# A22 copies in two PSUM banks by turns, block sums joined in SBUF ahead of the weight sums, later row sums, and regrouped last rows

## The chip, the core and the metric

The kernel runs on one core of one Trainium2 chip. The metric is the device time of one execution in microseconds; the kernel before takes 2215.24 us, the median of three runs. TensorE is called PE, VectorE DVE, ScalarE ACT, GpSimd POOL and SyncE SP. Every matmul operand is float32, cut into a rounded high part and a low part (the rest), and each product is three matmuls: high by high, low weight by high, high weight by low.

## The reference, cut to what matters

Two layers over 512 tokens of width 1024. Each layer has two gated feed-forward blocks (FFN) around a mixing stage; the FFNs are what the change touches.

```python
def swiglu(x, w_in, w_out):
    a, b = jnp.split(x @ w_in, 2, axis=-1)
    return (jax.nn.silu(a) * b) @ w_out

for l in range(DEPTH):                      # DEPTH = 2
    h = h + 0.5 * swiglu(rmsnorm(h, ffn1_norm[l]), ffn1_w_in[l], ffn1_w_out[l])   # D_FF = 2816
    u = rmsnorm(h, mix_norm[l])
    ...                                     # three branches, one of them attention into mem
    y_c = mem_attention(q_c, rmsnorm(mem, mem_norm[l]), w_mem_kv[l])
    ...
    h = h + 0.5 * swiglu(rmsnorm(h, ffn2_norm[l]), ffn2_w_in[l], ffn2_w_out[l])
return rmsnorm(h, final_norm)
```

## The kernel before, in words

**Pairs.** An FFN computes its 22 hidden tiles of 128 (both halves, so 44 units of weights) and its output as a list of 30 pairs, FLOW. A pair of kind "S" (four, at the front) is computed the standard way: two units of 24 matmuls over 512 tokens. The other 26 are computed by a fast product of 2 x 2 blocks: seven block products of 12 matmuls over 256 tokens each, 84 matmuls in all, in the order of PRODUCTS: A11, A12, S2, S1, S3, A22, S4. The A's are quarters of the weights and the S's are sums of quarters. Kind "K" is a hidden tile, kind "O" two output tiles whose result is added to h. The order is 4 S, 4 K of group A, 1 K of group C, 4 O, 8 K of group B, 1 K of C, 4 O, 4 K of C. The hidden tiles of groups A and B go in couples (tile t and tile t + 4, which I call near and far): their sums, sumS, are what the O pairs multiply. The last six hidden tiles (group C) are multiplied in the standard way by outs(), eight units of 18 matmuls over 512 tokens, into bank[k % 4].

**Windows.** PE runs pair after pair. On ACT and DVE, window(last, now, then) holds what belongs beside pair now: the end of pair last, the middle of now, and the weights of then. What stands in a window is in program order; all waits are on semaphores. In DVE's window: finish_blocks(last) (block sums from bank[1..3] into obank and bank[3], and the scaling by rms), then gate(last) or add_rows(last), then low_late A22 (the low part of now's A22 weights), low(last), low_late S4, sum_two and sum_four (weight sums of then), mix_first(now) (the first block sums of now, in obank and ta), low_s2, add_mem (only in the first FFN of a layer, after an O pair: squares of mem are added up), mix_two(now), couple_sums(last).

**Banks and who waits for them.** PE may begin the next pair's A11 and A12 when mix_first has read bank[0] and bank[1] (semaphore mixed), S1 when finish_blocks has read bank[2] (crossed), A22 when low(last) or add_rows is done (pair_done). The quarter A22 of the coming pair is copied by ACT into the PSUM bank tbank (copy_a22, line 1491), where sum_two and the rounding and low part of A22 read it; the copy waits for late_low, that is for both low_late steps of the pair before, since they read the bank.

**POOL and SP.** For every fast pair POOL makes two weight sums and four low parts (lines 842, 836, 848, 836), and after each second tile of a couple two low parts of the couple's sums (line 859). SP loads the quarters in the order A11, A12, A21, A22; A12 waits for sum_four.

**Last rows.** After outs() unit k, DVE's last_row(k) adds the result to h, makes the low part for the next stage, copies the row back to h and adds its square, which ACT makes, to ssq. norm_mem and low_mem (mem for the memory attention) stand after row 0 and row 1. PE's units k + 4 and, after them, the memory units wait for the bank of row k.

## Time and profile before

| | before |
|---|---|
| median of 3 runs | 2215.24 us (2213.0 to 2216.5) |
| profiled execution | 2214.67 us |
| span in the profile | 2212.9 us |
| granted clock of TensorE, mean | 0.992 |
| PE busy | 2141.6 us, 97% of the span |
| PE weight loads busy | 1928.8 us, 87% |
| DVE busy | 1678.9 us, 76% |
| POOL busy | 1490.8 us, 67% |
| ACT busy | 1068.6 us, 48% |
| DMA | 213.18 MB, mean 96 GB/s |

The table says how full each engine is over the whole program. The profile's waits say on whom PE waited, and the rows in order of time say how long one window of DVE is compared with one pair of PE. The stage from 56 to 341 us is the first FFN of layer 0 with its fast pairs, 802 to 1072 us its second FFN; the last rows of the first FFN lie from 341 to 394 us, and layer 1 repeats all of it some 1093 us later.

### The profile page before, as it was taken

The numbers are of one execution on the slowest core, as the hardware profiler recorded it, in microseconds if no ns is written. First come the engines' busy times: TensorE is split into PE (matmuls) and PEld (weight loads), VectorE is DVE, ScalarE is ACT, GpSimd is POOL, SyncE is SP. The second block draws the span as 40 slices with busy tenths as digits, with TensorE's granted clock in tenths as the row PEclk, the third lists the DMA queues.
The fourth block names the chain that finished last, engine by engine and source line by source line (L and its number), as shares of the span: only waits on it lengthen the run. The fifth ranks groups of instructions, "written<-read, shape, count | busy, mean of one in ns | idle before, by whom it ended". The sixth has DMA issues, their size and how long they took to land. (4 is left out here: it accounts for less than half of the span.)

```text
span 2212.9 us, 39425 instructions
## 1 busy us (share of the span) xinstructions
PE 2141.6 (97%) x13990; PEld 1928.8 (87%) x13990; DVE 1678.9 (76%) x3116; ACT 1068.6 (48%) x2067; POOL 1490.8 (67%) x1094
## 2 busy tenths in 40 slices
PE   9999998999999999999999999989999999999997
PEld 6999997788888889999879999968788888999996
DVE  6888887568765588888778888865787555888884
ACT  5545542444554255564345455434445533555552
POOL 6877866544445678788768788765444466788874
PEclk9999999999999999999999999999999999999999
DMA  5332333322222323333323233332222133232232
GB/s 167 108 109 92 115 106 110 116 70 67 72 63 77 106 85 101 107 99 101 109 82 117 96 101 114 109 121 93 69 63 72 54 108 96 81 111 97 98 104 85
DMA packets 95235, 213.18 MB, mean 96 GB/s; under 512 B 10400, under 2 KB 13640, under 8 KB 94792
## 3 DMA queue, kind: packets, MB, share of 16 engines
q1 hardware_dynamic: 90864, 205.42, 28.7%
q10 hardware_dynamic: 4184, 5.31, 0.7%
q8 instruction: 112, 1.84, 0.3%
q14 instruction: 75, 0.61, 0.1%
HBM read 208.58 MB, written 3.68 MB: 96 GB/s over the span
## 5 line engine op out<-in xcount | busy, mean ns | idle before, releaser
L791 POOL TENSOR_SCALAR wH<-raw 128x1024 fp32r<-128x1024 f32 (+2 forms) x184 | 173.4, 942 | 422.3 <-PE bank L921 352.3
L794 POOL TENSOR_TENSOR wL<-raw,wH 128x1024 fp32r<-128x1024 f32 (+2 forms) x184 | 389.1, 2115 | 15.3
L1051 PE MATMUL bank<-u1H,wH 128*128 128x256 f32 x1152 | 330.8, 287 | 10.3 <-DVE far4L L2031 6.3
L1052 PE MATMUL bank<-u1H,wL 128*128 128x256 f32 x1152 | 327.1, 284 | 0.0
L1053 PE MATMUL bank<-u1L,wH 128*128 128x256 f32 x1152 | 327.0, 284 | 0.0
L836 POOL TENSOR_TENSOR wL<-wS,wH 128x512 fp32r<-128x512 f32 x208 | 273.1, 1319 | 74.3 <-ACT wH L1497 39.3
L836 POOL TENSOR_TENSOR wL<-raw,wH 128x512 fp32r<-128x512 f32 x208 | 280.5, 1369 | 2.2 <-ACT wH L1503 2.1
L919 PE MATMUL bank<-u1H,wH 128*128 128x512 f32 x704 | 281.6, 400 | 0.0
L920 PE MATMUL bank<-u1H,wL 128*128 128x512 f32 x704 | 275.0, 391 | 0.0
L921 PE MATMUL bank<-u1L,wH 128*128 128x512 f32 x704 | 274.8, 390 | 0.0
L1051 PE MATMUL bank<-u0H,wH 128*128 128x256 f32 x864 | 248.3, 287 | 9.4 <-DVE ta L1959 9.1
L1052 PE MATMUL bank<-u0H,wL 128*128 128x256 f32 x864 | 244.4, 283 | 0.0
L1053 PE MATMUL bank<-u0L,wH 128*128 128x256 f32 x864 | 244.3, 283 | 0.0
L1051 PEld LDWEIGHTS bank<-u1H,wH 128*128 128x128 f32 x1152 | 222.1, 193 | 16.0 <-DVE far4L L2031 7.1
L1052 PEld LDWEIGHTS bank<-u1H,wL 128*128 128x128 f32 x1152 | 222.3, 193 | 0.0
L1053 PEld LDWEIGHTS bank<-u1L,wH 128*128 128x128 f32 x1152 | 222.1, 193 | 0.0
L842 POOL TENSOR_TENSOR wS<-raw 128x512 f32<-128x512 f32 x104 | 134.9, 1297 | 107.9 <-issue 89.5
L1051 PEld LDWEIGHTS bank<-u0H,wH 128*128 128x128 f32 x864 | 165.4, 191 | 16.8 <-DVE ta L1959 16.0
L1503 ACT ACTIVATE wH<-raw 128x512 fp32r<-128x512 f32 x208 | 130.3, 629 | 84.8 <-PE bank L1053 84.8
L1052 PEld LDWEIGHTS bank<-u0H,wL 128*128 128x128 f32 x864 | 165.6, 192 | 0.1
L1053 PEld LDWEIGHTS bank<-u0L,wH 128*128 128x128 f32 x864 | 165.5, 192 | 0.0
L919 PEld LDWEIGHTS bank<-u1H,wH 128*128 128x128 f32 x704 | 132.4, 188 | 33.4 <-issue 7.4
(332 smaller groups left out, 6113.4 us busy)
## 6 DMA issues: line engine op xcount, KB each, us to landing
raw<-in_wA SPq DMA_DIRECT2D x296, 256.0 KB, 2.9
raw<-in_wM SPq DMA_DIRECT2D x96, 512.0 KB, 3.5
raw<-in_wO SPq DMA_DIRECT2D x128, 256.0 KB, 2.9
raw<-in_wA SPq DMA_DIRECT2D x28, 512.0 KB, 3.6
raw<-in_wC SPq DMA_DIRECT2D x32, 384.0 KB, 3.0
raw<-in_wR SPq DMA_DIRECT2D x32, 256.0 KB, 2.6
keep<-in_memT SPq DMA_DIRECT2D x4, 512.0 KB, 3.3
mem<-in_memT SPq DMA_DIRECT2D x2, 1024.0 KB, 7.5
```

The lines of the kernel that those rows point to most:

```text
L791: pool.tensor_scalar(wH[:, w, 0:cols], raw[:, slot, 0:cols], 1.0, 0.0, ALU.mult, ALU.add).then_inc(rounded, 1)
L794: pool.tensor_tensor(wL[:, w, 0:cols], raw[:, slot, 0:cols], wH[:, w, 0:cols].bitcast(F32), ALU.subtract).then_inc(split_done, 1)
L836: pool.tensor_tensor(half_slot(wL_flat, n), full, half_slot(wH_flat, n).bitcast(F32), ALU.subtract).then_inc(pool_low, 1)
L842: pool.tensor_tensor(half_slot(wS, weights_at("S3", g)), quarter("A11"), quarter("A21"), ALU.subtract).then_inc(pool_sum, 1)
L919: pe.matmul(dst, a, hi[:, k, :], start=first and i == 0, stop=False)
L920: pe.matmul(dst, b, hi[:, k, :], start=False, stop=False)
L921: mm = pe.matmul(dst, a, lo[:, k, :], start=False, stop=last and i == len(tiles) - 1)
L1051: pe.matmul(dst, a, hi, start=begin and k == 0, stop=False)
L1052: pe.matmul(dst, b, hi, start=False, stop=False)
L1053: mm = pe.matmul(dst, a, lo, start=False, stop=end and k == 3)
L1503: act.activation(half_slot(wH_flat, weights_at(name, g)), quarter(name), ACT.Copy).then_inc(k_rounded, 1)
```

## The change

It does five things.

1. copy_a22 copies into tbank for even pairs and into obank for odd ones (a22_bank). The copy waits only for the A22 low part of the pair two before, and stands earlier in ACT's window, ahead of high(last) and copy_first(now).
2. Block sums are joined in SBUF. copy_first writes to sg instead of ta; mix_first is one operation over 512 columns into ta instead of two over 256 into obank and ta; finish_blocks sums one half into ta (SBUF), multiplies ta by rms there, and makes both crossed halves with one operation over two banks (banks_two). bank[2] and bank[3] change places: S1 and S3 go to bank[3], A22 and S4 to bank[2].
3. mix_first comes ahead of sum_two and sum_four in DVE's window.
4. A near tile stays in sumS itself, and the couple's sums are three operations instead of four. They stand ahead of low_s2. Those of the four standard pairs come in the windows at positions 3 and 4, and their high and low parts at 4 and 5.
5. In last_row the square of row k - 1 is added after the first operation of row k (add_square); norm_mem comes after row 1 instead of 0, low_mem after row 3 instead of 1, and ACT's parts of them after rows 1 and 2. A wait of PE on k_scaled is dropped.

```diff
+def couples_due(now, last):
+    if now is not None and now.pos in (4, 5):
+        return [FLOW[2 * (now.pos - 4) + 1]]
+    return [last] if last is not None and last.kind == "K" and last.group in "AB" and last.at >= 4 else []
...
         def kept(p):
-            return keep[:, p.at // 4, :]
+            return keep[:, p.at % 2, :] if p.at >= 4 else sumS[:, 2 * p.at, :]
+
+        def a22_bank(g):
+            return (tbank, obank)[g % 2]
...
-        bank = [ctx.enter_context(nc.psum_tensor(f"bank{i}", [P, 512], F32)) for i in range(BANKS)]
+        bank = [ctx.enter_context(nc.psum_tensor(f"bank{i}", [P, 512], F32)) for i in range(BANKS - 2)]
+        banks_two = ctx.enter_context(nc.psum_tensor("banks_two", [P, 2, 512], F32))
+        bank += [banks_two[:, i, :] for i in range(2)]
...
                         act.wait_ge(quarter_landed["A22"], 16 * (g + 1))
-                        act.wait_ge(late_low, 2 * g)
-                        act.activation(tbank[:, :], quarter("A22"), ACT.Copy).then_inc(a22_copied, 1)
+                        if g >= 2:
+                            act.wait_ge(late_low, 2 * (g - 2) + 1)
+                        act.activation(a22_bank(g)[:, :], quarter("A22"), ACT.Copy).then_inc(a22_copied, 1)
...
-                        act.activation(ta[:, 0:TH], bank[0][:, 0:TH], ACT.Copy).then_inc(first_copied, 1)
+                        act.activation(sg[:, 0, 0:TH], bank[0][:, 0:TH], ACT.Copy).then_inc(first_copied, 1)
...
                         if seven_then:
                             round_quarter(then, "A12")
+                            copy_a22(then)
                         if last is not None and last.kind != "O":
                             high(last)
                         if seven_now:
                             copy_first(now)
                         if seven_then:
-                            copy_a22(then)
                             round_sum(then, "S3")
...
-                        own.done(dve.tensor_tensor(obank[:, 0:TH], bank[1][:, 0:TH], ta[:, 0:TH], ALU.add))
-                        dve.tensor_tensor(ta[:, TH:T], bank[1][:, TH:T], ta[:, 0:TH], ALU.add).then_inc(mixed, 1)
+                        dve.tensor_tensor(halves(ta[:, :]), halves(bank[1][:, :]), twice(sg[:, 0, 0:TH]), ALU.add
+                                          ).then_inc(mixed, 1)
...
-                        own.done(dve.tensor_tensor(obank[:, TH:T], bank[3][:, TH:T], sg[:, 1, 0:TH], ALU.add))
-                        own.done(dve.tensor_tensor(bank[3][:, 0:TH], bank[3][:, 0:TH], sg[:, 1, TH:T], ALU.add))
+                        own.done(dve.tensor_tensor(ta[:, TH:T], bank[2][:, TH:T], sg[:, 1, 0:TH], ALU.add))
                         own.wait()
+                        scaled_rows = dve.tensor_tensor(ta[:, :], ta[:, :], rms[:, :], ALU.mult)
...
-                        dve.tensor_tensor(bank[3][:, TH:T], bank[2][:, 0:TH], sg[:, 1, TH:T], ALU.add
+                        dve.tensor_tensor(halves(bank[2][:, :]), banks_two[:, :, 0:TH], twice(sg[:, 1, TH:T]), ALU.add
                                           ).then_inc(crossed, 1)
...
-                        for i, made in ((0, obank), (1, bank[3])):
+                        for i, made in ((0, ta), (1, bank[2])):
...
+                        near, cross, own_two = sumS[:, 2 * j, :], sumS[:, 2 * j + 1, :], kept(p)
                         if p.at < 4:
-                            dve.tensor_tensor(sumS[:, 2 * j, left], keep[:, 0, right], keep[:, 0, left], ALU.subtract
+                            dve.tensor_tensor(near[:, left], near[:, right], near[:, left], ALU.subtract
                                               ).then_inc(couple_sum, 1)
                             return
-                        dve.tensor_tensor(sumS[:, 2 * j + 1, right], keep[:, 1, right], keep[:, 0, right], ALU.subtract
+                        dve.wait_ge(couple_sum, n + 1)
+                        dve.tensor_tensor(halves(cross), twice(own_two[:, right]), halves(near), ALU.subtract
                                           ).then_inc(couple_sum, 1)
-                        dve.tensor_tensor(sumS[:, 2 * j + 1, left], keep[:, 1, right], sumS[:, 2 * j, left], ALU.subtract
-                                          ).then_inc(couple_sum, 1)
...
+                        if seven_now:
+                            mix_first(now)
                         if seven_then:
                             sum_two(then)
                             sum_four(then)
-                        if seven_now:
-                            mix_first(now)
+                        if now is not None and now.pos in (3, 4):
+                            for p in FLOW[2 * (now.pos - 3):2 * (now.pos - 3) + 2]:
+                                couple_sums(p)
+                        if last is not None and last.kind == "K" and in_couple(last):
+                            couple_sums(last)
                         if seven_then:
                             low_s2(then)
...
-                        if last is not None and in_couple(last):
-                            couple_sums(last)
...
-                    finish_h(k, bank[k % BANKS][:, :], sbank[k % 2][:, :], 0.5, l * 24 + k + (n_from + 1), g, hi, lo)
+                    dve.scalar_tensor_tensor(ps, ps, 0.5, h[:, k, :], ALU.mult, ALU.add).then_inc(h_added, 1)
+                    if k:
+                        add_square(k - 1, n - 1)
```

The order on DVE in one window after an O pair, in the first FFN of layer 0, before (bank3, bank2: the PSUM banks; sbank0 and sbank1 hold weight sums):

```order
L1975 TENSOR_TENSOR obank<-bank3,sg 128x256
L1976 TENSOR_TENSOR bank3<-bank3,sg 128x256
L1981 TENSOR_TENSOR obank<-obank,rms 128x512
L1982 TENSOR_TENSOR bank3<-bank2,sg 128x256
L1989 TENSOR_TENSOR bank3<-bank3,rms 128x512
L1993 SCALAR_TENSOR_TENSOR h<-obank,h 128x512
L1993 SCALAR_TENSOR_TENSOR h<-bank3,h 128x512
L1938 TENSOR_TENSOR wL<-tbank,wH 128x512
L1938 TENSOR_TENSOR wL<-sbank1,wH 128x512
L1916 TENSOR_TENSOR sbank0<-tbank,wS 128x512
L1924 TENSOR_TENSOR sbank1<-raw,sbank0 128x512
L1958 TENSOR_TENSOR obank<-bank1,ta 128x256
```

And the same window in the changed kernel:

```order
L1989 TENSOR_TENSOR ta<-banks_two,sg 128x256
L1991 TENSOR_TENSOR ta<-ta,rms 128x512
L1996 TENSOR_TENSOR banks_two<-banks_two,sg 128x512
L2003 TENSOR_TENSOR banks_two<-banks_two,rms 128x512
L2007 SCALAR_TENSOR_TENSOR h<-ta,h 128x512
L2007 SCALAR_TENSOR_TENSOR h<-banks_two,h 128x512
L1952 TENSOR_TENSOR wL<-obank,wH 128x512
L1952 TENSOR_TENSOR wL<-sbank1,wH 128x512
L1972 TENSOR_TENSOR ta<-bank1,sg 128x512
L1930 TENSOR_TENSOR sbank0<-tbank,wS 128x512
L1938 TENSOR_TENSOR sbank1<-raw,sbank0 128x512
L1945 TENSOR_TENSOR wL<-sbank0,wH 128x512
```

The block sum of the current pair (L1958, now L1972) has moved ahead of the two weight sums, the operations of a window are two fewer, and two of them (L1991 and the first L2007) now have both inputs in SBUF.

The order on ACT from the first rounding of a window to the copy of the first block, after a far tile (raw: the quarters as loaded; wH: rounded weights), before:

```order
L1517 ACTIVATE wH<-tbank 128x512
L1503 ACTIVATE wH<-raw 128x512
L1523 ACTIVATE sg<-ta 128x512
L1517 ACTIVATE wH<-sbank1 128x512
L1503 ACTIVATE wH<-raw 128x512
L1537 ACTIVATE far4H<-keep 128x512
L1530 ACTIVATE ta<-bank0 128x256
L1491 ACTIVATE tbank<-raw 128x512
```

And in the changed kernel:

```order
L1530 ACTIVATE wH<-tbank 128x512
L1516 ACTIVATE wH<-raw 128x512
L1537 ACTIVATE sg<-ta 128x512
L1530 ACTIVATE wH<-sbank1 128x512
L1516 ACTIVATE wH<-raw 128x512
L1504 ACTIVATE obank<-raw 128x512
L1551 ACTIVATE far4H<-keep 128x512
L1544 ACTIVATE sg<-bank0 128x256
```

The copy of A22 (L1491, now L1504) has moved ahead of the rounding of the hidden tile (far4H) and of the block copy.

The order on DVE over the first last rows of layer 0's first FFN, before:

```order
L2124 TENSOR_TENSOR ssq<-sbank0,ssq 128x512
L1832 SCALAR_TENSOR_TENSOR obank<-obank,mem_rms 128x256
L1834 SCALAR_TENSOR_TENSOR obank<-obank,mem_rms 128x256
L1836 SCALAR_TENSOR_TENSOR mem_rms<-obank,mem_rms 128x256
L2136 TENSOR_TENSOR mem<-mem,mem_rms 128x256 x8
L2116 SCALAR_TENSOR_TENSOR bank1<-bank1,h 128x512
L2119 SCALAR_TENSOR_TENSOR u1L<-bank1,pr,u1H 128x512
L2121 COPY h<-bank1 128x512
L2124 TENSOR_TENSOR ssq<-sbank1,ssq 128x512
L2146 SCALAR_TENSOR_TENSOR yL<-mem,pr,yH 128x256 x8
```

And in the changed kernel:

```order
L2146 SCALAR_TENSOR_TENSOR bank1<-bank1,h 128x512
L2160 TENSOR_TENSOR ssq<-sbank0,ssq 128x512
L2151 SCALAR_TENSOR_TENSOR u1L<-bank1,pr,u1H 128x512
L2153 COPY h<-bank1 128x512
L1846 SCALAR_TENSOR_TENSOR obank<-obank,mem_rms 128x256
L1848 SCALAR_TENSOR_TENSOR obank<-obank,mem_rms 128x256
L1850 SCALAR_TENSOR_TENSOR mem_rms<-obank,mem_rms 128x256
L2168 TENSOR_TENSOR mem<-mem,mem_rms 128x256 x8
```

Row 1 (bank1) now stands ahead of the scaling of mem, and the square of row 0 is added inside row 1.

## Rows read from the trace of the kernel before

**Rows 1.** The page, busy us and share of the span, each engine.

```profile
PE 2141.6 (97%) x13990; PEld 1928.8 (87%) x13990; DVE 1678.9 (76%) x3116; ACT 1068.6 (48%) x2067; POOL 1490.8 (67%) x1094
```

**Rows 2.** The waits of PE's weight loads, whole program: us in total, times, longest.

```profile
PEld bank L1051 <- DVE ta L1959: 24.6, 48, 0.7
PEld bank L1112 <- DVE h L2121: 11.1, 6, 3.7
...
PEld bank L1051 <- DVE bank L1982: 7.7, 23, 0.9
PEld bank L1051 <- DVE far4L L2031: 7.1, 4, 2.9
...
PEld bank L1166 <- POOL wL L794: 5.4, 1, 5.4
PEld bank L1051 <- POOL sumL L859: 4.8, 8, 1.1
...
PEld bank L1051 <- DVE earlyL L2028: 2.9, 8, 0.4
```

**Rows 3.** Two stretches by engine: length, then busy us (count) of PE, PEld, DVE, ACT, POOL.

```profile
897.20:907.30 10.10, 10.10 (x87) 10.10 (x86) 8.41 (x15) 4.81 (x9) 7.88 (x7) 1.00 0.35 114
157.10:168.30 11.20, 10.68 (x85) 10.25 (x85) 9.79 (x17) 5.14 (x11) 7.64 (x6) 1.00 0.28 94
```

**Rows 4.** DVE in order of time, one window after an O pair: start, us, line.

```profile
159.94 0.43 DVE L1975 TENSOR_TENSOR obank<-bank,sg 128x256 f32<-128x256 f32 x1
...
166.05 0.70 DVE L1916 TENSOR_TENSOR sbank<-tbank,wS 128x512 f32<-128x512 f32 x1 [0.79 <-POOL wS L848]
...
169.06 1.32 DVE L2057 TENSOR_TENSOR mem_rms<-keep,mem_rms 128x256 f32<-128x256 f32 x1
...
171.09 0.43 DVE L1975 TENSOR_TENSOR obank<-bank,sg 128x256 f32<-128x256 f32 x1
```

**Rows 5.** ACT in order of time, the same window.

```profile
165.36 0.60 ACT L1491 ACTIVATE tbank<-raw 128x512 f32<-128x512 f32 x1 [4.07 <-DVE wL L1938]
```

**Rows 6.** DVE in order of time, starts of three K windows of that FFN.

```profile
181.55 0.42 DVE L1975 TENSOR_TENSOR obank<-bank,sg 128x256 f32<-128x256 f32 x1
...
193.61 0.42 DVE L1975 TENSOR_TENSOR obank<-bank,sg 128x256 f32<-128x256 f32 x1
...
203.26 0.42 DVE L1975 TENSOR_TENSOR obank<-bank,sg 128x256 f32<-128x256 f32 x1
```

**Rows 7.** DVE in order of time, second FFN, starts of two windows after O pairs.

```profile
897.41 0.43 DVE L1975 TENSOR_TENSOR obank<-bank,sg 128x256 f32<-128x256 f32 x1 [0.22 <-PE bank L1053]
...
907.49 0.43 DVE L1975 TENSOR_TENSOR obank<-bank,sg 128x256 f32<-128x256 f32 x1 [0.50 <-PE bank L1053]
```

**Rows 8.** Groups by line: busy us, mean ns of one, idle before.

```profile
L2057 DVE TENSOR_TENSOR mem_rms<-keep,mem_rms 128x256 f32<-128x256 f32 x14 | 18.4, 1316 | 1.9
L1979 DVE TENSOR_TENSOR ta<-obank,rms 128x512 f32<-128x512 f32 x72 | 49.8, 691 | 2.5
```

**Rows 9.** POOL in order of time, the window of rows 4.

```profile
160.55 1.29 POOL L842 TENSOR_TENSOR wS<-raw 128x512 f32<-128x512 f32 x1 [1.59 <-issue]
...
168.80 1.30 POOL L836 TENSOR_TENSOR wL<-wS,wH 128x512 fp32r<-128x512 f32 x1 [0.62 <-ACT wH L1497]
```

**Rows 10.** DVE in order of time, the last rows of layer 0's first FFN.

```profile
356.35 6.26 DVE L2136 TENSOR_TENSOR mem<-mem,mem_rms 128x256 f32<-128x256 f32 x8 [0.21 <-DVE mem_rms L1836]
362.53 0.69 DVE L2116 SCALAR_TENSOR_TENSOR bank<-bank,h 128x512 f32<-128x512 f32 x1
...
378.12 0.69 DVE L2116 SCALAR_TENSOR_TENSOR bank<-bank,h 128x512 f32<-128x512 f32 x1
379.64 0.75 DVE L2119 SCALAR_TENSOR_TENSOR u1L<-bank,pr,u1H 128x512 fp32r<-128x512 f32 x1 [0.83 <-ACT u1H L1609]
...
381.65 0.69 DVE L2124 TENSOR_TENSOR ssq<-sbank,ssq 128x512 f32<-128x512 f32 x1 [0.67 <-ACT sbank L1612]
382.26 0.69 DVE L2116 SCALAR_TENSOR_TENSOR bank<-bank,h 128x512 f32<-128x512 f32 x1
```

More of the change, by code:

```diff
@@ L874, in ffn_units @@
                             k_weights(f, p)
-                        before = FLOW[p.pos - 2] if p.pos >= 2 else None
-                        if before is not None and in_couple(before) and before.at >= 4:
-                            couple_lows(f, before)
+                        if p.pos > 0:
+                            for q in couples_due(FLOW[p.pos - 1], FLOW[p.pos - 2] if p.pos > 1 else None):
+                                couple_lows(f, q)
                     first = u_first[f] + OUT_UNIT
@@ L998, in mixed_bank @@
                     def mixed_bank(b, n):
-                        pe.wait_ge({0: mixed, 1: mixed, 2: crossed, 3: pair_done}[b], n)
+                        pe.wait_ge({0: mixed, 1: mixed, 2: pair_done, 3: crossed}[b], n)
                     def bank_free(p, b):
@@ L1579, in window @@
                             round_sum(then, "S1")
-                        if last is not None and in_couple(last) and last.at >= 4:
-                            couple_highs(last)
+                        for p in couples_due(now, last):
+                            couple_highs(p)
                         if last is not None and last.kind == "O" and f == 0:
```

78 lines of the change are left out of this document (45 added, 33 removed).

## The prediction, made before the changed kernel ran

> **What bounds the kernel now.** The page first: PE is busy 97% of the span, DVE 76%, POOL 67% [rows 1]. So what can be won is PE's waits, about 71 us (2212.9 less 2141.6), and only where a wait goes for good. Next the waits of the weight loads, which stop and start with PE's queue [rows 2]. Two places stand out. In the fast pairs (L1051) PE waits 24.6 us for mixed, 7.7 for crossed, 4.8 for the couples' low parts and 2.9 for a C pair's low part, 42 us with the smaller ones; 7.1 more fall on the first fast pair of each FFN. In the last rows of the first FFN it waits 11.1 us for evacuated rows and 5.4 at the memory units, which stands twice, once per layer under another name, so some 22 us.
>
> Then the windows in order of time. In step with PE, windows start 10.08 us apart and DVE still waits 0.22 and 0.50 us for PE [rows 7]; PE is never idle there, with DVE busy 8.41 of 10.10 us [rows 3]. That is one pair of PE, the floor. In the first FFN of a layer a window after an O pair lasts 171.09 - 159.94 = 11.15 us [rows 4], with DVE busy 9.79 of 11.20 and PE idle half a microsecond by its own row [rows 3]. Windows after K pairs take 193.61 - 181.55 = 12.06 and 203.26 - 193.61 = 9.65, on average 10.85 [rows 6]. So most of the fast pairs are bound by the length of DVE's window, not by PE. A part of an engine that is "only" 76% busy is the bound.
>
> A check of that reading. A window may start some 1.9 us late before PE stops (mixed comes 8.2 us behind its start, and PE wants it at 10.08). Per first FFN: 4 K windows gain 3.1 of lag, 1.2 past the 1.9; a C window gives 0.5 back; 4 O windows at +1.07 lose 3.8; 8 K windows at +0.77 lose 6.2; C and O again 3.8: 15.0 us. Per second FFN, where O windows are at the floor: 1.2 + (6.2 - 1.9) = 5.5. Twice both gives 41.0, against 42 in the rows. The count may be used on the change.
>
> **The change on DVE's window.** (a) The copy of A22 now waits 4.07 us on ACT for DVE's second low part [rows 5], and sum_two waits for the copy: 0.79 us idle [rows 4]. With two banks it is long done: -0.79 in each window. (b) Block sums: finish_blocks and mix_first lose two of six operations; an operation over 256 columns costs 0.34 to 0.46 from start to start and one over 512 about 0.61, so finish 1.91 to 1.76, mix 0.76 to 0.61: -0.30. (c) One couple add fewer per two windows: -0.22 in K windows. (d) mix_first ahead of the weight sums gives mixed some 1.5 us earlier, which raises the lag that PE tolerates for banks 0 and 1. But A22's bank then decides, freed by low(last) at 5.4 to 6.2 us for a want at 7.2, so I take a tolerance of 1.5 instead of 1.9. (e) mix_first no longer stands between sum_four and low_s2, which needs ACT to round sum two's result (0.60 and two hand-overs): +0.75 after O pairs; in K windows the couple adds fill it. (f) On ACT the copy (0.60) stands ahead of high(last), for which DVE's low(last) waits: +0.5 in K windows, nothing after O.
>
> (g) The scaling of ta, and in O windows h<-ta,h, now have both inputs in SBUF. The rows show what such an operation costs beside POOL: mem_rms<-keep,mem_rms, 256 columns, takes 1316 ns, while 256 columns with a PSUM input take 0.43 us [rows 4, 8]. At 169.06 POOL works from 168.80 on for 1.30 us, and DVE's operation ends at 170.38, 0.28 after POOL's [rows 4, 9]. ta<-obank,rms with its PSUM input takes 691 ns over 72 of them, beside POOL or not [rows 8]. So the bounds of one added operation are 0 (POOL idle, or DVE first) and 1.29 (it starts just after POOL did). POOL is busy 7.64 of 11.20 us here [rows 3]: half of an operation at 68% is 0.44. The scaling comes 0.5 us into the window, where POOL's first sum starts at 160.55, 0.6 us in, behind a pause of 1.59 [rows 9]. I take 0.3 for it, and 0.6 for h<-ta,h, which lies amid POOL's run. In K windows 0.3, and 0.2 for the couple add that is now 512 wide.
>
> The Trainium skill, page "SBUF — State Buffer", section "SBUF: two separate sides", says that a DVE operation with two SBUF inputs and a POOL operation that reads SBUF take one port pair as an exclusive lock, first come, and the other fully blocks. The trace agrees: 1316 ns against 691 for twice the columns with a PSUM input. It speaks against the joining in SBUF, and is the mechanism of rival 4.
>
> Sums. K windows: 10.85 - 0.79 - 0.30 - 0.22 + 0.5 + 0.5 = 10.54. O windows with add_mem: 11.15 - 0.79 - 0.30 + 0.75 + 0.9 = 11.71; part of this will overlap, since a later start meets POOL's pauses, and I take 11.4. O windows of the second FFN: 11.4 less the 1.57 that add_mem costs (11.15 - 9.58, the 10.08 less 0.50 idle [rows 7]), under the floor. The same count with tolerance 1.5: first FFN 0.4 + 4.9 + 3.8 + 4.8 = 13.9, second 0.4 + (3.7 - 1.5) = 2.6; twice both 33. Against 41 that is **-8 us**. The couples' sums come earlier by low_s2 and mix_two (1.2 us); of the 4.8 us for sumL half goes: **-2**.
>
> **First fast pairs.** There the wait for far4L (7.1 us, four times) [rows 2] lies behind the low part of the last standard pair. Its rounding on ACT now comes after a copy that needs the next pair's A22 landed, 0.6 to 1, and window 3 has three couple adds instead of one. Between 0 and +6; I take **+3.5**. Windows 1 and 2 lose adds, which PE's standard pairs hide.
>
> **The last rows.** A row takes DVE 382.26 - 378.12 = 4.14 us, of which 0.83 waiting for ACT's high part and 0.67 for its square [rows 10]; PE gives a unit about as fast. With the square of row k - 1 in the first gap both waits shrink: 0.61 + 0.61 + 0.3 + 0.67 + 0.61 = 2.8 us a row. Before, row 1 comes at 362.53 because of mem (6.26) [rows 10], and each later row keeps that lag, up to the memory units. Now row 1, which comes ahead of mem's scaling, is done near 355 (356.35 less the three operations and waits that it swaps places with), mem's scaling ends at 362 to 365.4 (8 operations: 2.7 us at 0.34, or 6.3 as in the row, by POOL's hold), rows 2 and 3 and low_mem take until 373.5 to 376.5 (row 3 behind ACT's eight operations on mem, some 3 us), and rows 4 to 7 at 2.9 end at 385 to 388, not 393.4: -5.4 to -8.4 per layer. Middle, twice: **-14**. Late next would be the memory units' weights on POOL, for which PE waits little now (its row names POOL, but the second layer's, at the same place and length, names nobody).
>
> Sum: -8 - 2 + 3.5 - 14 = -20.5. The profiled execution took 2214.67 us (0.57 under the median), so 2194; on the median 2194.7.
>
> **The rivals.** 1. Forecast: windows stay the bound, last rows win: 2195. 2. The two SBUF operations fall into POOL's pauses, h<-ta,h too, and windows come under the floor: of 42 us nearly all go, with last rows at -15 and first pairs at +3: 2215 - 40 - 15 + 3 = 2163. For it: POOL's pause of 1.59 stands just ahead of the scaling, and the second FFN already runs at the floor. Against: K windows. 3. Windows come out as long as now (collisions 0.1 to 0.3 above what I took): only the last rows and nothing else, 2215 + 3 - 11 = 2207. 4. Last rows win 5 us, and that is eaten by longer windows: within 0.2%, 2214; so also if a PE wait is handed to POOL or DMA, that the copies don't touch. 5. Slower: the scaling of ta meets POOL in every window. The mechanism feeds itself, because POOL's first sum starts a fixed time behind DVE's sum_four, by the load that waits for it, and so always 0.5 us into the next window. A full 1.29 instead of 0.3 in half of the 80 K and O windows is +40: 2235. It decides from 20.5/80 = 0.26 us a window above what I took. For it: add_mem waits the same 0.9 each of 14 times (1316 ns mean, close to the single 1.32) [rows 4, 8], so phases do lock.
>
> **How the numbers follow.** Chances: forecast 0.42, rival 2 0.22, rival 3 0.13, rival 4 0.08, rival 5 0.15. A measurement of this kernel tells about 0.2% (4.4 us) from no change. Faster 0.77, same 0.08, slower 0.15. The range takes in rivals 2 and 3 with their bounds (low: 2163 with last rows at -17 and first pairs at 0, 2158) and rival 4 at the top, 2217; it leaves out rival 5 and the far ends.
>
> **What would show it.** Right: no idle ahead of sum_two; last rows 2.8 to 3 us apart and the memory units' 5.4 us wait gone; ta<-ta,rms with a mean between 0.8 and 1.1 us; O windows of first FFNs still over 11 us. Wrong: a scaling at 0.69 throughout and pairs at 10.08 everywhere (rival 2), or at 1.3 and more, with PE's waits for crossed or pair_done grown past 40 us (rival 5); or a first fast pair that waits over 4 us.

## The result, and the profile after

The changed kernel takes 2256.2 us, the median of 4 runs (2252.2 to 2262.2), against 2214.1 for the kernel before beside it: ratio 1.0196, 95% interval 1.0165 to 1.0227. It is slower by 42 us, where 2195 was forecast, and lies outside the range of 2158 to 2217. Its profiled execution took 2252.22 us, with a span of 2250.4 and a mean granted clock of 0.989 (before 0.992).

The page of the changed kernel, busy us and share of the span, answers [rows 1]:

```profile
PE 2144.9 (95%) x13990; PEld 1932.5 (86%) x13990; DVE 1779.6 (79%) x2876; ACT 1059.7 (47%) x2067; POOL 1531.5 (68%) x1094
```

DVE has 240 instructions fewer and is busy 100.7 us longer than before. So its operations got slower, not more. PE's busy time rose by 3.3 us only (2144.9 less 2141.6), so nearly all of the loss is time in which PE waits. The waits of PE's weight loads (us in total, times, longest), after, to be laid beside [rows 2]:

```profile
PEld banks_two L1064 <- DVE banks_two L1996: 41.2, 38, 2.0
PEld banks_two L1064 <- DVEq L2009: 10.1, 11, 1.2
PEld banks_two L1064 <- DVE far4L L2045: 8.5, 4, 2.6
PEld bank L1166 <- issue: 7.9, 1, 7.9
```

The wait for mixed (24.6 us before) is gone, as planned. The wait for crossed (L1996; L1982 before) went from 7.7 to 41.2, and pair_done of the O pairs (L2009) is new. In what follows, SBUF is the on-chip memory of the tiles ta, keep, sumS, rms, h and mem, and PSUM the banks (bank, banks_two, obank, tbank, sbank). DVE in order of time, after: a window behind an O pair, to [rows 4], and the starts of three K windows, to [rows 6] (start, duration in us, line; in brackets, where it stands, the idle time ahead of the operation and what ended it):

```profile
164.86 0.42 DVE L1989 TENSOR_TENSOR ta<-banks_two,sg 128x256 f32<-128x256 f32 x1
165.32 1.57 DVE L1991 TENSOR_TENSOR ta<-ta,rms 128x512 f32<-128x512 f32 x1
...
168.28 1.55 DVE L2007 SCALAR_TENSOR_TENSOR h<-ta,h 128x512 f32<-128x512 f32 x1
169.76 0.68 DVE L2007 SCALAR_TENSOR_TENSOR h<-banks_two,h 128x512 f32<-128x512 f32 x1
...
175.39 1.31 DVE L2071 TENSOR_TENSOR mem_rms<-keep,mem_rms 128x256 f32<-128x256 f32 x1
...
177.41 0.42 DVE L1989 TENSOR_TENSOR ta<-banks_two,sg 128x256 f32<-128x256 f32 x1
177.87 0.69 DVE L1991 TENSOR_TENSOR ta<-ta,rms 128x512 f32<-128x512 f32 x1
```

```profile
187.32 0.42 DVE L1989 TENSOR_TENSOR ta<-banks_two,sg 128x256 f32<-128x256 f32 x1
...
198.83 0.42 DVE L1989 TENSOR_TENSOR ta<-banks_two,sg 128x256 f32<-128x256 f32 x1
...
209.69 0.43 DVE L1989 TENSOR_TENSOR ta<-banks_two,sg 128x256 f32<-128x256 f32 x1
```

The O window lasts 12.55 us (before 11.15, forecast 11.4). The scaling takes 1.57 there and the first row of h 1.55, while the second row, which reads its first input from PSUM, takes 0.68. The K windows take 11.19 on average (before 10.85, forecast 10.54). This O window is one of the longest: the scaling of the next one (177.87) takes 0.69. Over all windows of a kind, read the same way from the two traces, the 16 O windows of the first FFNs went from 11.13 to 11.91 us on average, the 48 windows behind a K pair of groups A and B from 10.74 to 11.20, the 8 behind the first two C pairs of each FFN from 10.35 to 10.60, and the O windows of the second FFNs stayed at 9.8. The groups by line (busy us, mean ns of one, then idle before), after:

```profile
L1991 DVE TENSOR_TENSOR ta<-ta,rms 128x512 f32<-128x512 f32 x104 | 102.4, 985 | 3.6
...
L1945 DVE TENSOR_TENSOR wL<-sbank,wH 128x512 fp32r<-128x512 f32 x104 | 71.3, 685 | 31.9 <-ACT wH L1523 31.9
...
L2057 DVE TENSOR_TENSOR sumS<-keep,sumS 128x512 f32<-128x512 f32 x32 | 45.0, 1406 | 0.3
L2007 DVE SCALAR_TENSOR_TENSOR h<-ta,h 128x512 f32<-128x512 f32 x32 | 40.0, 1250 | 1.1
...
L2060 DVE TENSOR_TENSOR sumS<-keep,sumS 128x256 f32<-128x256 f32 x32 | 34.1, 1066 | 1.1
L2053 DVE TENSOR_TENSOR sumS<-sumS 128x256 f32<-128x256 f32 x32 | 33.1, 1035 | 0.0
L2042 DVE TENSOR_TENSOR far4L<-keep,far4H 128x512 fp32r<-128x512 f32 x24 | 32.1, 1338 | 3.3 <-ACT far4H L1551 1.3
L2042 DVE TENSOR_TENSOR near4L<-sumS,near4H 128x256 fp32r<-128x256 f32 x24 | 30.4, 1266 | 1.8 <-ACT near4H L1551 1.7
```

Every operation shown here that grew has both inputs in SBUF. The same groups of the kernel before, which stand nowhere ahead of the prediction:

```profile
L2028 DVE TENSOR_TENSOR far4L<-keep,far4H 128x512 fp32r<-128x512 f32 x24 | 26.6, 1109 | 2.5 <-ACT far4H L1537 0.2
L2041 DVE TENSOR_TENSOR sumS<-keep 128x256 f32<-128x256 f32 x32 | 25.6, 799 | 0.0
...
L2043 DVE TENSOR_TENSOR sumS<-keep,sumS 128x256 f32<-128x256 f32 x32 | 18.7, 584 | 0.0
...
L2038 DVE TENSOR_TENSOR sumS<-keep 128x256 f32<-128x256 f32 x32 | 17.7, 552 | 0.0
...
L2028 DVE TENSOR_TENSOR near4L<-keep,near4H 128x256 fp32r<-128x256 f32 x24 | 17.3, 720 | 0.0
...
L2046 DVE TENSOR_TENSOR sumS<-keep,sumS 128x256 f32<-128x256 f32 x32 | 13.6, 425 | 1.1
```

The couples' sums went from 75.6 us (25.6 + 18.7 + 17.7 + 13.6) to 112.2, although there is one operation fewer in each couple, and these low parts from 43.9 to 62.5. The change gave none of them a second SBUF input: it moved them.

The last rows after, DVE in order of time, to [rows 10]:

```profile
372.64 7.48 DVE L2168 TENSOR_TENSOR mem<-mem,mem_rms 128x256 f32<-128x256 f32 x8 [0.21 <-DVE mem_rms L1850]
...
387.45 0.75 DVE L2151 SCALAR_TENSOR_TENSOR u1L<-banks_two,pr,u1H 128x512 fp32r<-128x512 f32 x1 [3.18 <-ACT u1H L1623]
...
388.71 9.11 DVE L2178 SCALAR_TENSOR_TENSOR yL<-mem,pr,yH 128x256 fp32r<-128x256 f32 x8
...
400.52 0.69 DVE L2146 SCALAR_TENSOR_TENSOR bank<-bank,h 128x512 f32<-128x512 f32 x1
...
403.30 0.69 DVE L2146 SCALAR_TENSOR_TENSOR banks_two<-banks_two,h 128x512 f32<-128x512 f32 x1
```

The rows do run 2.78 us apart. But low_mem, eight operations on SBUF alone, takes 9.11 us (3.24 before, at its old place), and row 3 waits 3.18 for ACT, which the prediction had at some 3.

### The profile page after: what moved, and what is told of

It reads as the page before. It is cut to its first block, busy times and chain, and to the rows that moved or that the text cites. A ratio compares the mean times of both kernels' runs of the same rounds, so it can differ in the third digit from the quotient of the medians.

```text
span 2250.4 us, 39175 instructions
## 1 busy us (share of the span) xinstructions
PE 2144.9 (95%) x13990; PEld 1932.5 (86%) x13990; DVE 1779.6 (79%) x2876; ACT 1059.7 (47%) x2067; POOL 1531.5 (68%) x1094
## 4 chain that ended last, share of the span: by engine, by line
PE 65%; DVE 23%; issue 5%; ACT 5%; DMA 1%; POOL 1%; DVEq 0%; SPq 0%; ACTq 0%; POOLq 0%
PE bank L932 6%; PE bank L933 6%; PE bank L934 6%; PE banks_two L1064 5%; PE banks_two L1065 5%; PE banks_two L1066 5%; PE banks_two L932 4%; PE banks_two L934 4%; PE banks_two L933 4%; PE bank L1066 3%; PE bank L1064 3%; PE bank L1065 3%; DVE ta L1991 3%; DVE wL L1952 2%; DVE sumS L2057 1%
## 5 line engine op out<-in xcount | busy, mean ns | idle before, releaser
L1064 PE MATMUL banks_two<-u1H,wH 128*128 128x256 f32 x864 | 253.9, 294 | 41.4 <-DVE banks_two L1996 22.7
L1065 PE MATMUL banks_two<-u1H,wL 128*128 128x256 f32 x864 | 247.3, 286 | 0.0
L1066 PE MATMUL banks_two<-u1L,wH 128*128 128x256 f32 x864 | 247.1, 286 | 0.0
L855 POOL TENSOR_TENSOR wS<-raw 128x512 f32<-128x512 f32 x104 | 142.8, 1373 | 137.5 <-issue 88.5
L1064 PEld LDWEIGHTS banks_two<-u1H,wH 128*128 128x128 f32 x864 | 168.4, 195 | 53.8 <-DVE banks_two L1996 27.3
L932 PE MATMUL bank<-u1H,wH 128*128 128x512 f32 x480 | 191.2, 398 | 0.0
L1065 PEld LDWEIGHTS banks_two<-u1H,wL 128*128 128x128 f32 x864 | 168.6, 195 | 0.0
L1066 PEld LDWEIGHTS banks_two<-u1L,wH 128*128 128x128 f32 x864 | 168.5, 195 | 0.0
L861 POOL TENSOR_TENSOR wS<-raw 128x512 f32<-128x512 f32 x104 | 145.0, 1394 | 10.3 <-PE banks_two L1066 9.4
L1510 ACT ACTIVATE wH<-wS 128x512 fp32r<-128x512 f32 x208 | 129.8, 624 | 11.9 <-POOL wS L861 9.7
L1064 PE MATMUL banks_two<-sumH,wH 128*128 128x256 f32 x384 | 111.6, 291 | 20.2 <-DVE banks_two L1996 10.9
```

The lines of the kernel that those rows point to most:

```text
L855: pool.tensor_tensor(half_slot(wS, weights_at("S3", g)), quarter("A11"), quarter("A21"), ALU.subtract).then_inc(pool_sum, 1)
L861: pool.tensor_tensor(half_slot(wS, weights_at("S1", g)), quarter("A21"), quarter("A22"), ALU.add).then_inc(pool_sum, 1)
L932: pe.matmul(dst, a, hi[:, k, :], start=first and i == 0, stop=False)
L1064: pe.matmul(dst, a, hi, start=begin and k == 0, stop=False)
L1065: pe.matmul(dst, b, hi, start=False, stop=False)
L1066: mm = pe.matmul(dst, a, lo, start=False, stop=end and k == 3)
```

## The experiments

The kernel before, run beside each group, had medians of 2213.4 to 2217.1 us; so a difference of two or three microseconds between runs of different groups says nothing. Two theories stood against each other. Theory 1: DVE operations with both inputs in SBUF wait for POOL, and that makes the windows long. Theory 2: the new order of the window (block sums first, low_s2 behind a wait for ACT) costs the time, whatever the operations last. A third cause, the place of low_mem, could stand beside either.

**The memory part back in its place.** In the changed kernel, rows left overlapped:

```diff
-                    if k == 1:
+                    if k == 0:
                         norm_mem()
-                    if k == 3:
+                    if k == 1:
                         low_mem()
```

(and ACT's parts alike).

> The changed kernel with norm_mem and low_mem back behind rows 0 and 1 of the last rows (and ScalarE's parts of them behind the same rows); the rows stay overlapped. Theory 3 (low_mem moved behind row 3 falls into GpSimd's run and takes 9.0 us where it took 3.2, which eats the gain of the overlapped rows): low_mem back to 3 to 4 us, the gaps of TensorE of 7.63 and 3.33 us around the rows gone in each of the two layers, so 10 to 14 us less than the changed kernel: 2242 to 2246. Rival (the rows wait for GpSimd or ScalarE anyway, and low_mem early only moves the same wait ahead): within 4 us of the changed kernel, 2252 to 2260.

2237.8 us, ratio to before 1.0109 (1.0093 to 1.0126): 18.4 less than the changed kernel, more than I gave it. Its DVE in order of time:

```profile
381.28 3.28 DVE L2178 SCALAR_TENSOR_TENSOR yL<-mem,pr,yH 128x256 fp32r<-128x256 f32 x8 [1.10 <-ACT yH L1638]
```

Behind row 3, low_mem had met POOL's split of the memory units' weights (in the changed kernel a run of 128x1024 operations from 389.12 to 397.14). Behind row 1 POOL is idle (5.65 us before its next, at 386.37), and the eight take 3.28 us.

**The order alone, on the kernel before.** No buffer or operation differs:

```diff
+                        if seven_now:
+                            mix_first(now)
                         if seven_then:
                             sum_two(then)
                             sum_four(then)
-                        if seven_now:
-                            mix_first(now)
+                        if last is not None and in_couple(last):
+                            couple_sums(last)
                         if seven_then:
                             low_s2(then)
...
-                        if last is not None and in_couple(last):
-                            couple_sums(last)
```

> The kernel before with only VectorE's order changed: mix_first ahead of sum_two and sum_four, and the couples' sums ahead of low_s2; no buffer, no input and no operation is different. Theory 1 (the two-SBUF operations are the loss, the order is harmless): the idle time of about 1.1 us ahead of sum_two in a K window is partly filled, 0 to 12 us less than before: 2202 to 2214. Theory 2 (the order is the loss: low_s2 then waits 0.66 us for ScalarE in O windows, and crossed and pair_done keep less room): 10 us or more slower than before, 2224 or above.

2241.9 us, 1.0122 (1.0106 to 1.0139): 27 slower. Read by the time alone this is theory 2, and a miss for theory 1 as I had put it ("the order is harmless"). But the trace says more. DVE's busy time rose from 1678.9 to 1737.9 us with the same 3116 instructions. Two groups of this run, then DVE and POOL in order of time inside one window:

```profile
L2046 DVE TENSOR_TENSOR sumS<-keep,sumS 128x256 f32<-128x256 f32 x32 | 41.0, 1280 | 1.1
...
L2028 DVE TENSOR_TENSOR near4L<-keep,near4H 128x256 fp32r<-128x256 f32 x24 | 32.9, 1372 | 0.0
```

```profile
91.83 0.98 DVE L2041 TENSOR_TENSOR sumS<-keep 128x256 f32<-128x256 f32 x1
92.73 0.41 DVE L2043 TENSOR_TENSOR sumS<-keep,sumS 128x256 f32<-128x256 f32 x1
93.18 1.55 DVE L2046 TENSOR_TENSOR sumS<-keep,sumS 128x256 f32<-128x256 f32 x1
```

```profile
91.23 1.30 POOL L836 TENSOR_TENSOR wL<-wS,wH 128x512 fp32r<-128x512 f32 x1 [1.08 <-DVE sbank L1916]
93.15 1.30 POOL L836 TENSOR_TENSOR wL<-wS,wH 128x512 fp32r<-128x512 f32 x1 [0.62 <-ACT wH L1497]
```

POOL's first operation ends at 92.53 and DVE's sum at 92.81; POOL's second ends at 94.45 and DVE's third sum at 94.73. Both end 0.28 us behind POOL's, wherever they began. The middle one fell into POOL's pause and took 0.41. This holds beyond the one window: of the 128 couples' sums of this run 41 take 0.41 to 0.43 us, and each of the other 87 ends 0.28 to 0.29 us behind an operation of POOL. Likewise in the changed kernel 60 of the 104 scalings take 0.69 us, and each of the other 44, twice as wide, ends 0.55 us behind one of POOL. So the order costs through what it puts beside POOL, which the next run tests.

**The same order, one input in PSUM.** The couples' sums read obank in place of their second SBUF input in the windows of fast pairs (and wait for mix_first, which writes it), so they hold other numbers:

```diff
-                        dve.tensor_tensor(sumS[:, 2 * j, right], keep[:, 1, left], sumS[:, 2 * j + 1, left], ALU.subtract
+                        second = obank[:, left] if seven else sumS[:, 2 * j + 1, left]
+                        dve.tensor_tensor(sumS[:, 2 * j, right], keep[:, 1, left], second, ALU.subtract
```

(and the other three alike).

> The kernel of e3_order_only in which the couples' sums take their second input from the bank obank in PSUM in place of keep or sumS in SBUF, in the windows of pairs that take seven products (so the couples' sums hold other numbers; place, size and count of the operations stay). In e3_order_only these sums, moved ahead of low_s2 into GpSimd's run, take 1280, 997, 902 and 551 ns, where before they took 425, 799, 552 and 584. Theory 1 (an operation with both inputs in SBUF waits for the end of GpSimd's operation, and that is why the place matters): all four at 420 to 450 ns, the waits of TensorE for crossed at L1982 fall from 37.5 us to under 12, and the time comes to 2192 to 2212, below e3_order_only by 30 to 50 us. Theory 2 (the order itself makes the window long, through the wait of 0.66 us ahead of low_s2 and the lost room behind it): the sums shorten, but the time stays within 10 us of e3_order_only, 2232 to 2242.

2191.1 us, 0.9895 (0.9878 to 0.9912): 51 less than the order alone, and 25 less than before. Two of its four groups:

```profile
L2053 DVE TENSOR_TENSOR sumS<-keep,obank 128x256 f32<-128x256 f32 x28 | 11.8, 422 | 1.0
...
L2042 DVE TENSOR_TENSOR sumS<-keep,obank 128x256 f32<-128x256 f32 x24 | 10.0, 415 | 0.0
```

At the same place, 1280 ns became 422. None of the 108 sums that read obank took more than 0.43 us, though POOL was at work when 80 of them began. The same order that costs 27 us with two inputs in SBUF costs nothing with one in PSUM, and theory 2 falls. The 25 us below the kernel before are not the order's alone: there, too, the sums had met POOL (75.6 us against 55.0 here), and that kernel with obank as their input in the old place was not run.

**Block sums first, nothing else.** In the kernel before, mix_first ahead of the weight sums, the couples' sums left behind mix_two.

> The kernel before with only mix_first moved ahead of sum_two and sum_four; the couples' sums stay behind mix_two. Theory 1 (the loss of e3_order_only is the couples' sums in GpSimd's run): the idle time ahead of sum_two moves ahead of low_s2 and little changes, within 8 us of before, 2207 to 2223. Theory 2 (mix_first ahead takes room from the sums and so from low_s2, crossed and pair_done): most of the 27 us of e3_order_only appear, 2230 to 2242.

2209.7 us, 0.997 (0.996 to 0.998): 6 less than before, theory 1. The idle time of DVE moves from sum_two to low_s2:

```profile
L1916 DVE TENSOR_TENSOR sbank<-tbank,wS 128x512 f32<-128x512 f32 x104 | 72.7, 699 | 12.6 <-issue 0.5
...
L1931 DVE TENSOR_TENSOR wL<-sbank,wH 128x512 fp32r<-128x512 f32 x104 | 71.9, 692 | 69.1 <-ACT wH L1510 69.1
```

Before, these were 79.2 and 3.5 us.

**The rows alone, and the rows with either order.**

> The kernel before with only the overlapped last rows of the layers, norm_mem and low_mem where they were. From e3_order_only to e4_order_rows the rows gave 20.4 us; here the same, 2192 to 2198, if the rows and the FFN's windows are independent (theory 1 and theory 2 agree). If the gain hangs on the order in the window ahead of them, over 2202.

> The kernel before with the order of e3_order_only, and the overlapped last rows (the square of row k added behind row k+1), with norm_mem and low_mem left behind rows 0 and 1. My account of the last rows (2.8 us from row to row in place of about 4, and low_mem still ahead of GpSimd's run): 7 us in each of two layers and about 4 between the layers on top of e3_order_only, so 15 to 19 less than it: 2183 to 2199 under theory 1. If the rows' gain is met by a wait for GpSimd anyway, less than 6 us below e3_order_only.

> The kernel before with the overlapped last rows and mix_first ahead of the weight sums, and nothing else of the change. The rows gave 21.7 us, mix_first 6.4; they lie in different stretches, so the sum under theory 1: 2184 to 2192. If both live on the same wait (theory 2, the room in the windows decides about the rows too): no better than e7_rows_only, 2192 or above.

The overlapped rows alone on the kernel before: 2194.3 us, 0.9910 (0.9893 to 0.9927), 21.7 less. On top of the order with the couples' sums: 2221.5 us, 1.0031 (1.0021 to 1.0041), 20.4 less than without the rows (my figure for the time, 2183 to 2199, missed with that order; the difference came out a little above the 15 to 19 expected). With mix_first: 2191.9 us, 0.9886 (0.9869 to 0.9903), at the upper end of what I expected; of mix_first's 6 us two or three are left, which these runs don't separate from nothing.

**The changed kernel with the joined sums read from PSUM.** The scaling and the first row of h read a bank in PSUM in place of ta, so the sums that ta holds are left out of the result; number, place and size of the operations stay.

```diff
-                        scaled_rows = dve.tensor_tensor(ta[:, :], ta[:, :], rms[:, :], ALU.mult)
+                        scaled_rows = dve.tensor_tensor(ta[:, :], bank[3][:, :], rms[:, :], ALU.mult)
...
-                        for i, made in ((0, ta), (1, bank[2])):
+                        for i, made in ((0, bank[2]), (1, bank[2])):
```

> The changed kernel in which the scaling by rms reads the bank of S1 in PSUM, and the first row of h the bank of A22, in place of ta in SBUF (so the own block sums that ta holds are left out of the gate and of h; number, place and size of the operations stay). Theory 1: the scaling falls from 985 ns to about 700 in 104 pairs (30 us of VectorE), the first row of h from 1250 to about 700 in 32 pairs (18 us); where TensorE waits for crossed and pair_done this comes back nearly one for one: 2221 to 2240. Theory 2 (the order): both shorten, the time stays above 2246.

2208.3 us, 0.9967 (0.9955 to 0.998): 48 less than the changed kernel, below my range. Its groups:

```profile
L1991 DVE TENSOR_TENSOR ta<-banks_two,rms 128x512 f32<-128x512 f32 x104 | 71.9, 692 | 3.6
...
L2007 DVE SCALAR_TENSOR_TENSOR h<-banks_two,h 128x512 f32<-128x512 f32 x64 | 41.3, 686 | 1.1
```

The scaling gives back 102.4 - 71.9 = 30.5 us and the first rows of h 18 (32 at 1250 less 686 ns), 48.5 in all. The time fell by as much, which is partly chance: some 6 of the 48.5 lie in the O windows of the second FFNs, which PE bounds anyway. The couples' sums (110.4 us) and the low parts (57.2) stay almost as slow as in the changed kernel.

**The couples' sums back, in the changed kernel.** The block of couple_sums moved behind mix_two(now), nothing else.

> The changed kernel with the couples' sums back behind mix_two (the standard pairs' too, in the same windows), all else as changed. They take 1406, 1066 and 1035 ns in 32 each (112 us); at their old place those of before took 425 to 799. Theory 1: they fall to 450 to 900 ns, 25 to 55 us of VectorE's time in 64 windows; against it stands that nothing fills the 0.66 us ahead of low_s2 any more. Sum 10 to 30 us less than the changed kernel: 2226 to 2246. Theory 2 (place is indifferent, the added room ahead of low_s2 is what the change won): 2256 to 2280.

2276.9 us, 1.0258 (1.0236 to 1.0280): 21 slower than the changed kernel. Theory 1's number was wrong here, in sign too, and the time lies in the range written down for the other theory. Two rows of it:

```profile
L1991 DVE TENSOR_TENSOR ta<-ta,rms 128x512 f32<-128x512 f32 x104 | 117.0, 1125 | 3.6
...
L1945 DVE TENSOR_TENSOR wL<-sbank,wH 128x512 fp32r<-128x512 f32 x104 | 71.9, 692 | 69.1 <-ACT wH L1523 69.1
```

The sums fell only to 91 us (41.2 + 29.4 + 20.4). Against these 21 stand 37 us of idle time ahead of low_s2 (31.9 to 69.1), which they had filled, and 15 us more in the scaling. The theory that the added room ahead of low_s2 is what the change had won was right about these 37 us; that the place is indifferent to the sums was not (112.2 to 91 us). A sum beside POOL cannot be moved as if the others stayed where they are.

**One bank for A22, in the changed kernel.** a22_bank returns tbank, with the wait of one pair; first with ACT's copy where the change has it (ahead of high), then with the copy back behind high and copy_first.

> The changed kernel with the copies of A22 in one bank (tbank), all else as changed. My step (a) gave the two banks 0.79 us in each window, the idle time ahead of sum_two; if it is theirs, this kernel is 30 to 60 us slower than the changed one, 2286 to 2316. Rival: the move of mix_first fills that idle time by itself (as in e3_order_only, where it is gone with one bank), and the second bank brings nothing: within 5 us of the changed kernel, 2251 to 2261.

> e12_one_bank with ScalarE's copy of A22 back behind high and copy_first. In e12_one_bank nothing waited ahead of sum_two, but the single bank made ScalarE wait ahead of high, and VectorE's low waited 96 us for it, so that run did not price my step (a). Here low has nothing to wait for. If step (a) was right (0.79 us in each window belong to the second bank), 30 to 60 us slower than the changed kernel, 2286 to 2316, with idle time ahead of sum_two. Rival (mix_first ahead of the weight sums covers the copy; the second bank brings nothing): within 6 us of the changed kernel, 2250 to 2262, and no idle time ahead of sum_two.

The first took 2319.8 us, 1.0457 (1.0438 to 1.0475), just above the range that I had for "the second bank is worth it". It did not show that. Nothing waits ahead of sum_two; it is the low parts of the hidden rows that wait for ACT, which itself waits 226.1 us ahead of the copy for DVE's low part of A22:

```profile
L2042 DVE TENSOR_TENSOR near4L<-sumS,near4H 128x256 fp32r<-128x256 f32 x24 | 31.8, 1327 | 25.8 <-ACT near4H L1551 25.8
L2042 DVE TENSOR_TENSOR far4L<-keep,far4H 128x512 fp32r<-128x512 f32 x24 | 27.3, 1137 | 30.7 <-ACT far4H L1551 30.7
```

The second took 2255.6 us, 1.0189 (1.0169 to 1.0208), the changed kernel's time. Its row for sum_two has no idle time:

```profile
L1930 DVE TENSOR_TENSOR sbank<-tbank,wS 128x512 f32<-128x512 f32 x104 | 71.3, 686 | 0.0
```

With mix_first ahead of the weight sums one bank with the late copy does as well as two with the early one, and the second bank is what drove the block sums out of obank into SBUF. Bank and place of the copy change together here; two banks with the late copy were not run. In the profiled executions the equality is a sum of two parts: the first fast pairs of the FFNs are 6.4 us shorter with one bank and the late copy, the other fast pairs 6.4 us longer.

**Both causes taken away.**

> e8_psum_in and e2_mem_back together: the changed kernel with the scaling and the first row of h read from PSUM (ta's own block sums left out of the gate and of h), and norm_mem and low_mem back behind rows 0 and 1. The two gave 48 and 18.4 us alone; if they are independent and are the whole of my error, 2186 to 2194, at my forecast of 2195. If they share a wait, one of them is given back: over 2198.

2189.8 us, 0.9887 (0.9871 to 0.9904): 66.4 less than the changed kernel, the sum of 48 and 18.4, so the two causes are independent. That this lies near my forecast of 2195 is chance. The forecast had priced the two SBUF inputs (0.3 us in a window, 0.9 behind an O pair), which this run takes away whole, and had not priced the slower couples' sums and low parts, which it keeps.

**A version that beats both.** The overlapped rows and mix_first on the kernel before, and the mechanism used on add_mem, the operation with two SBUF inputs that [rows 8] show at 1316 ns:

```diff
+                        if last is not None and last.kind == "O" and f == 0 and last.at:
+                            add_mem(last)
                         if seven_then:
                             low_s2(then)
-                        if last is not None and last.kind == "O" and f == 0:
+                        if last is not None and last.kind == "O" and f == 0 and not last.at:
                             add_mem(last)
```

(on ACT the squaring of the piece goes ahead of the copy of A22; 14 of the 16 windows with add_mem are moved).

> e9_rows_mix with add_mem (mem_rms<-keep,mem_rms, both inputs in SBUF, 1316 ns where its [128, 256] of PSUM take 425) ahead of low_s2, in the idle time of 0.66 us there, and ScalarE's squaring of the piece ahead of its copy of A22, in 14 of the 16 windows. Theory 1 says that an operation with two SBUF inputs costs the rest of GpSimd's operation, wherever it stands: started behind sum_four it waits about 0.6 us for GpSimd, under which the wait for low_s2 is hidden, and a window of the first FFNs falls from 11.15 to at most 10.4 us, that is 0.7 to 1.07 in 14 windows, 8 to 14 us less than e9_rows_mix: 2172 to 2182. Rival: the phase of GpSimd's run moves along with the shorter window and other operations with two SBUF inputs pay: less than 4 us.

2174.9 us, 0.9805 (0.9788 to 0.9822): 42 less than before, and 17 less than without it, where 8 to 14 was expected. DVE in order of time:

```profile
149.02 0.43 DVE L1977 TENSOR_TENSOR obank<-bank,sg 128x256 f32<-128x256 f32 x1
...
156.56 0.98 DVE L2059 TENSOR_TENSOR mem_rms<-keep,mem_rms 128x256 f32<-128x256 f32 x1
157.47 0.68 DVE L1933 TENSOR_TENSOR wL<-sbank,wH 128x512 fp32r<-128x512 f32 x1
...
158.85 0.43 DVE L1977 TENSOR_TENSOR obank<-bank,sg 128x256 f32<-128x256 f32 x1
```

add_mem still waits for POOL (0.98 us where one beside no POOL operation takes 0.43), but in time that DVE had to wait for ACT anyway; the window is 9.83 us, under PE's 10.08, where [rows 4] had 11.15.

A kernel in which POOL's own work is taken away was not tried. That POOL is the other party rests on the ends, which fall 0.28 or 0.55 us behind POOL's in every long operation counted above, and on the PSUM inputs that end the delay.

## Why the prediction was wrong, point by point

- **What bounds the kernel** was read rightly: DVE's window in the fast pairs. The windows grew by 0.78 us (the 16 O windows of the first FFNs, mean) and 0.46 us (the 48 K windows of groups A and B), and the time by 42 us; 48.5 us off DVE's operations came back as 48. The check by counting lag gave 41 us for the kernel before, where the starts of the fast pairs give 47.7 behind the first; its C window "gives 0.5 back", but takes 10.35 us and gives nothing.
- **Where the time went, by the terms of the sum.** From the starts of the fast pairs in the two profiled executions: the fast pairs behind the first of each FFN +31.6 us, forecast -8 and -2; the first fast pairs +7.4, forecast +3.5; the stretch from the last fast pair of a first FFN to the second FFN, which holds the last rows, +1.4 in layer 0 and 0 in layer 1, forecast -14 for both; the same behind layer 0's second FFN -4.1, not in the sum; the start +1.2. Together +37.5, where -20.5 was forecast.
- **(a) the second bank.** The idle time ahead of sum_two went, as said. But it went through (d), mix_first, in the same gap; I credited the bank with it, and then charged (e) for its return ahead of low_s2. In O windows the two cancel: 0.79 less there, 0.66 more here. Bank and early copy together are worth 0 (2255.6 without them).
- **(b), (c)** block sums: fewer operations as counted, worth 0.21 to 0.23 us a window for 0.30. **The credit of 0.22 for the couples' sums was the failing step in K windows, and the largest:** I priced them and the low parts at their old durations in new places. Over the 48 K windows the sums went from 1.07 to 1.74 us a window, start to start, and the low parts from 0.84 to 1.23: +1.06, where -0.22 and the 0.2 of (g) were all that I had. The window of 10.54 measured 11.20 us. (f), 0.5 for ACT's copy, is nearly absent (1.3 and 1.7 us of idle time over 48 windows).
- **(g) the two new SBUF operations.** The means were right: 0.29 for the scaling (985 against 691 ns; 0.3 forecast) and 0.56 for h (0.6). In the O windows of the first FFNs, where DVE has no room, they cost more: 0.40 for the scaling (9 of 16 at 0.69, the others 1.45 to 1.77) and 0.73 for h, 1.13 for my 0.9. With that, 11.13 - 0.79 - 0.30 + 0.75 + 1.13 = 11.92, against 11.91 measured. What failed here is the step from 11.71 down to 11.4: the 0.3 that I took off for overlap was hope without a row.
- **Fast pairs:** the starts of the fast pairs, each less the one before and less 10.08, add up to 97.4 us after and 58.4 before. Of these +39 the first pair of each FFN has 7.4. The rest is +31.6 instead of -10, and mostly in the waits for crossed that rival 5 named (41.2 us, past its mark of 40). Rival 5 had the sign, the mechanism and the place that stalls, at a chance of 0.15. Its other mark, a scaling at 1.3 and more, did not come (985 ns). It looked only at ta, so its price, 2235, was low.
- **First fast pairs:** the four together last 18.1 us longer than four times 10.08, before 10.6: +7.4 for my +3.5. Their low parts last nearly as before (near4L 1255 and 1254 ns, far4L 979 and 904), and PE's wait for far4L rose only from 7.1 to 8.5 us. But behind that wait PE ran at a granted clock of 0.50 for some 3 us in three of the four, where before it was 1.00: 0.50 is the lower of its two levels, 1.2 GHz, and the matmuls there start 0.21 us apart and not 0.12. One stretch after and one before, in layer 0's second FFN, columns as in [rows 3] with the granted clock behind POOL's:

```profile
824.20:825.20 1.00, 0.82 (x4) 0.82 (x5) 1.00 (x3) 0.00 (x0) 1.00 (x1) 0.50 0.51 88
808.00:809.00 1.00, 0.85 (x7) 0.85 (x8) 0.70 (x2) 0.21 (x1) 1.00 (x1) 1.00 0.00 0
```

- **The cause of that** is likely the copy ahead of high, which I had priced, though too low: with the copy back behind high, and one bank, the four are 11.7 us over and the clock in those three is 1.00. The copy's place was not tested by itself.
- **Last rows.** The overlap itself was right: alone it gave 21.7 us, in the profiled execution 8.8 and 8.0 in the last rows that the forecast of -14 was about, and 4.1 in those behind layer 0's second FFN, where the forecast had not looked. The step that failed is low_mem "until 373.5 to 376.5": I took its length from its old place. In the new one it takes 9.11 us and not 3.24, and the 8.8 and 8.0 are gone (+1.4 and 0). With mem back in its place they return, and the kernel is 18.4 us faster. The waits at the memory units that I said would vanish became 7.9 and 4.9 us.
- **The signs.** Four of the signs of being right came: no idle time ahead of sum_two, rows 2.78 us apart, a scaling of 985 ns on average, O windows over 11 us. The fifth, no wait at the memory units, failed, and was the only one that touched low_mem. None looked at a K window, where most of the loss in the fast pairs lay, so they could come with the time outside the range.
- **The rule of the Trainium skill** (page "SBUF — State Buffer", section "SBUF: two separate sides": a DVE operation with two SBUF inputs and a POOL operation that reads SBUF exclude each other for the whole instruction) is borne out: 1280 against 422 ns for one operation at one place. The prediction calls it the mechanism of rival 4; it is that of rival 5. I used it for the operations that the change adds, and should have used it for all that it moves.

## What to carry to other kernels

List every VectorE operation whose inputs both lie in SBUF, mark when GpSimd runs, and price each such operation that a change adds or moves at the rest of the GpSimd operation that it meets, in the windows where VectorE has no room, not by its mean over the program. A second buffer that pushes a result out of PSUM must be worth more than that; first try whether a change of order alone hides the wait. An operation that must collide is best put into time in which VectorE waits for something else.

## What the runs showed of the hardware

- What a collision costs is the rest of GpSimd's operation: an operation of 128x256 with two SBUF inputs took 0.41 us in POOL's pause and 0.98 or 1.55 us beside it, ending 0.28 us after POOL's operation each time (87 of 87 long ones in the order-only run). One of 128x512 took 0.69 alone and ended 0.55 us after POOL's (44 of 44 long scalings in the changed kernel). With one input in PSUM none of 108 operations of 128x256 took over 0.43 us, and the scaling of 128x512 took 0.69 us in each of its 104 (692 ns on average).
- It goes both ways: POOL's busy time rose from 1490.8 to 1531.5 us in the changed kernel at the same 1094 instructions, and fell to 1498.8 with the scaling and h read from PSUM.
